# Two stages of a two-layer encoder reordered: results of a Toeplitz convolution sent from ScalarE's queue, and an output projection split into 3 + 1 + 4 heads

## The reference

```python
def conv_module(x, w_pw1, b_pw1, w_dw, b_dw, ln_g, ln_b, w_pw2, b_pw2):
    h = x @ w_pw1 + b_pw1
    h = h[..., :D_MODEL] * jax.nn.sigmoid(h[..., D_MODEL:])
    h = lax.conv_general_dilated(
        h, w_dw[:, None, :], window_strides=(1,), padding=[(CONV_HALF, CONV_HALF)],
        dimension_numbers=('NWC', 'WIO', 'NWC'), feature_group_count=D_MODEL) + b_dw
    h = jax.nn.silu(layer_norm(h, ln_g, ln_b))
    return h @ w_pw2 + b_pw2
...
    def attend(blk):
        qn, qr = blk
        s = (jnp.einsum('bqhd,bkhd->bhqk', qn, k_nope, preferred_element_type=jnp.float32)
             + jnp.einsum('bqhr,bkr->bhqk', qr, k_rope, preferred_element_type=jnp.float32))
        p = jax.nn.softmax(s * scale, axis=-1).astype(v.dtype)
        return jnp.einsum('bhqk,bkhd->bqhd', p, v)

    o = lax.map(attend, (qn_blocks, qr_blocks))
    o = o.transpose(1, 0, 2, 3, 4).reshape(B, S, N_HEADS * V_HEAD_DIM)
    return o @ w_o
```

## Time and profile before

| what | value |
|---|---|
| median of three runs | 2750.94 us |
| the profiled execution | 2742.61 us |
| its span on the core | 2740.8 us |
| TensorE matmul busy | 2650.6 us, 97% |
| VectorE busy | 1399.2 us, 51% |
| ScalarE busy | 950.8 us, 35% |
| GpSimd busy | 1576.7 us, 58% |
| mean granted clock of TensorE | 0.992 |
| convolution stage | from 550 to 820 us, about |
| last head of attention | from 2121 to 2145 us, about |

### The profile page before, as it was taken

How to read it: one execution, slowest core, us unless ns; L and a number is a source line. 1 busy time by engine, 2 the same in 40 slices (tenths; PEclk the granted TensorE clock), 3 DMA queues, 4 the chain that set the end, 5 groups by cost and what they waited for, 6 DMA issues and landing times.

```text
span 2740.8 us, 36417 instructions
## 1 busy us (share of the span) xinstructions
PE 2650.6 (97%) x14320; PEld 2470.2 (90%) x14320; DVE 1399.2 (51%) x2533; ACT 950.8 (35%) x1580; POOL 1576.7 (58%) x852
## 2 busy tenths in 40 slices
PE   7999999899899999999999999999899999999998
PEld 7899999789778899999898999998899788999998
DVE  5643333669767643333664333337766476433335
ACT  4232332444243232332432322334444242323323
POOL 2576776657443576776636866674211234768665
PEclk9999999999899999999999999999999999999999
DMA  3222221322302222221421212241000121222213
GB/s 135 75 69 70 85 77 47 125 77 91 124 39 85 80 67 72 82 77 47 162 85 62 77 58 67 77 134 72 9 24 32 70 77 70 77 62 77 82 57 123
DMA packets 61944, 210.98 MB, mean 77 GB/s; under 512 B 8016, under 2 KB 11600, under 8 KB 61776
## 3 DMA queue, kind: packets, MB, share of 16 engines
q1 hardware_dynamic: 55536, 186.54, 20.3%
q10 hardware_dynamic: 6240, 22.12, 2.1%
HBM read 193.62 MB, written 12.58 MB: 75 GB/s over the span
## 4 chain that ended last, share of the span: by engine, by line
PE 82%; DVE 11%; issue 2%; ACT 2%; POOL 2%; SPq 1%; DMA 1%; DVEq 0%; ACTq 0%; POOLq 0%
PE ps L1073 27%; PE ps L1074 26%; PE ps L1075 26%; DVE raw_sum L1749 2%; DVE sum L1749 1%; POOL pacc L1060 1%; DVE x L1767 1%; PE ps L1173 1%; DVE y L1756 1%; POOL w_lo L1020 1%; SPq L909 1%; DVE y L1773 1%; PE ps L1320 1%; PE ps L1185 0%; DVE pair L1647 0%
## 5 line engine op out<-in xcount | busy, mean ns | idle before, releaser
L1020 POOL TENSOR_TENSOR w_lo<-w_stage,w_hi 128x1024 fp32r<-128x1024 f32 (+1 forms) x455 | 1020.3, 2271 | 595.7 <-ACT w_hi L1378 589.7
L1073 PE MATMUL ps<-xn,w_hi 128*128 128x384 f32 x1920 | 646.1, 336 | 11.1 <-DVE cin L1845 5.4
L1074 PE MATMUL ps<-xn,w_hi 128*128 128x384 f32 x1920 | 644.0, 335 | 0.0
L1075 PE MATMUL ps<-xn,w_lo 128*128 128x384 f32 x1920 | 643.5, 335 | 0.0
L1378 ACT ACTIVATE w_hi<-w_stage 128x1024 fp32r<-128x1024 f32 (+1 forms) x455 | 436.0, 983 | 84.6 <-POOL w_stage L1031 54.7
L1073 PE MATMUL ps<-w_hi,hid 128*128 128x512 f32 x1056 | 413.2, 391 | 4.9 <-DVE y L1761 3.4
L1074 PE MATMUL ps<-w_lo,hid 128*128 128x512 f32 x1056 | 411.8, 390 | 0.0
L1075 PE MATMUL ps<-w_hi,hid 128*128 128x512 f32 x1056 | 411.8, 390 | 0.0
L1073 PEld LDWEIGHTS ps<-xn,w_hi 128*128 128x128 f32 x1920 | 361.9, 188 | 14.6 <-issue 13.8
L1074 PEld LDWEIGHTS ps<-xn,w_hi 128*128 128x128 f32 x1920 | 362.0, 189 | 0.8
L1075 PEld LDWEIGHTS ps<-xn,w_lo 128*128 128x128 f32 x1920 | 361.8, 188 | 0.0
(11 more groups left out here) (198 smaller groups left out, 3928.8 us busy)
## 6 DMA issues: line engine op xcount, KB each, us to landing
w_stage<-weights SPq DMA_DIRECT2D x311, 512.0 KB, 3.6
x_kept<-x ACTq DMA_DIRECT2D x18, 512.0 KB, 2.6
x<-x_kept ACTq DMA_DIRECT2D x18, 512.0 KB, 7.3
g_pre<-rows SPq DMA_DIRECT2D x7, 512.0 KB, 4.7
spread_w<-spread_in SPq DMA_DIRECT2D x6, 576.0 KB, 4.4
late_spread_w<-spread_in SPq DMA_DIRECT2D x6, 576.0 KB, 4.7
x<-x_in SPq DMA_DIRECT2D x6, 512.0 KB, 8.3
g_post<-rows SPq DMA_DIRECT2D x6, 512.0 KB, 5.4
```

The lines of the kernel that those rows point to most:

```text
L1020: pool.tensor_tensor(w_lo[:, s, 0:n], w_stage[:, s, 0:n], w_hi[:, s, 0:n].bitcast(F32), ALU.subtract).then_inc(w_split, 1)
L1073: pe.matmul(out, a[0], m[0], start=start, stop=False)
L1074: pe.matmul(out, a[0], m[1], start=False, stop=False)
L1075: return pe.matmul(out, a[1], m[0], start=False, stop=stop)
```

## The change

Convolution. The clock `pool` now also advances by 2.6 for each split that falls inside an `up`, so products are placed later. The transfers of `bring` for chunks 5 and 7 become steps of the list (`bring c a`, right after `gather c a`) and are issued by ScalarE; SyncE keeps chunk 3 and, of chunk 7, group 2. SyncE requests the first four late matrices together and the other two after the first and second `send` of chunk 7.

Attention. The output projection has three blocks: heads 0 to 2, head 3, heads 4 to 7. Nine of its groups become steps of the last head and of what follows it; the rest comes after. The last head's keys and values lie on `last_kn` and `last_val`, over parts of `lat` that are no longer read and over `act_out`, so the weight places 4 to 6 come free after head 6. Groups before the last block use PSUM banks 2 and 3. The pre-norm row that shares its place with the last head's rotated queries is loaded ahead of row unit 7 instead of 4.

```diff
+HEAD_BLOCKS = ((0, 3), (3, 1), (4, 4))
...
+    return {"ffn": FFN_BLOCKS, "conv": ROW_BLOCKS, "mla": HEAD_BLOCKS}[SUBS[b]]
...
+    return LAST_BANKS[j] if last else (2 if SUBS[b] == "mla" else 4) + j % 2
...
         def item(c, half):
+            nonlocal pool
+            at_split = s.split
             up(b, c, half)
+            pool += 2.6 * (s.split - at_split)
             pool_until(s.clock)
...
                 if r % 2 == 1:
                     on_dve(0.8, "gather", c, r // 2)
+                    if c > SPREAD_CHUNKS[0]:
+                        s.add(0, "bring", c, r // 2)
...
-        s.add(0, "bring_last")
...
+            items = [(t, h) for t in range(TILES) for h in range(2)]
+            early = iter([(0, *at) for at in items[:8]] + [(1, *items[0])] + [
+                (n, *at) for two in zip(items[8:], items[1:5]) for n, at in enumerate(two)] + [
+                (1, *at) for at in items[5:]])
...
+                if n >= QK - 6:
+                    early_down()
                 if n >= 2:
                     s.add(0.4, "probs_turn", n - 2)
                 if n >= 5 and n % 2 == 1:
                     s.add(0.6, "value", (n - 5) // 2)
+                    if n == 5 + 2 * (3 * (HEADS - 1) - 1):
+                        for i in range(4, 7):
+                            s.free(UNIT0[b] + i, "attention", 3 * (HEADS - 1))
                 s.weights()
+            early_down()
             s.add(0.6, "value", QK // 2 - 1)
-            for i in range(4, 8):
-                s.free(UNIT0[b] + i, "attention", QK // 2)
-            s.weights(until=row_unit(b, 3))
-            for t in range(TILES):
-                for h in range(2):
-                    down(b, 0, t, h, 2 * t + h)
+            s.free(UNIT0[b] + 7, "attention", QK // 2)
+            for n, t, h in early:
+                down(b, n, t, h, next(placed))
...
+        last_kn = over("last_kn", [P, 2, TOK], spot["y"] + LAT * TOK * 4, F32R)
+        last_val = [over("last_val_hi", [P, TILES, VDIM], spot["y"] + (LAT + 2) * TOK * 4, F32R),
+                    over("last_val_lo", [P, TILES, VDIM], spot["act_out"], F32R)]
...
-                    load_spread(6)
-                    load_spread(7)
+                    for g in range(LATE, GROUPS - 2):
+                        load_spread(g)
                     for r in range(PHASES):
                         send(7, r)
-                        load_spread(8 + r)
-                    bring(5)
+                        if r < 2:
+                            load_spread(GROUPS - 2 + r)
                     bring(7)
...
                 e = SPREAD_CHUNKS.index(c)
-                for a in range(2):
+                for a in range(2) if c == SPREAD_CHUNKS[0] else (1,):
                     sp.wait_ge(gathered, 2 * e + a + 1)
-                    for r in (2 * a, 2 * a + 1):
-                        if (c, r) == (KT - 1, PHASES - 1):
-                            return
+                    for r in (2 * a, 2 * a + 1) if c == SPREAD_CHUNKS[0] else (PHASES - 2,):
...
-            def bring_last():
-                act.wait_ge(gathered, 2 * len(SPREAD_CHUNKS))
-                for q in range(PHASES):
-                    act.dma_start(out_place(KT - 1, PHASES - 1, q), sums_out(KT - 1)[quarter(q), PHASES - 1, :]
-                                  ).then_inc(brought[-1], 16)
+            def bring(c, a):
+
+                e = SPREAD_CHUNKS.index(c)
+                act.wait_ge(gathered, 2 * e + a + 1)
+                for r in (2 * a, 2 * a + 1):
+                    if (c, r) == (KT - 1, PHASES - 2):
+                        continue
+                    for q in range(PHASES):
+                        act.dma_start(out_place(c, r, q), sums_out(c)[quarter(q), r, :]).then_inc(brought[e], 16)
```

More of the change, by code:

```diff
@@ L1 @@
 from contextlib import ExitStack
+from itertools import count
 import concourse.bass as bass
@@ L196, with out_bank @@
 LAST_BANKS = (4, 5, 0, 1, 4, 5, 0, 1, 2, 3, 4, 5)
-def out_bank(last, j):
-    return LAST_BANKS[j] if last else 4 + j % 2
+def out_bank(b, last, j):
+    return LAST_BANKS[j] if last else (2 if SUBS[b] == "mla" else 4) + j % 2
 def turn_bank(t):
@@ L816, in qr, with keys_of, values_of @@
             return xn[rows_, i, h + 1, cols_] if h + 1 < HEADS else qr7[i][rows_, cols_]
+        def keys_of(h, i):
+            return last_kn[:, i, :] if h == HEADS - 1 else kn[:, h % 2, i, :]
+        def values_of(h, i):
+            return last_val[i][:, :, :] if h == HEADS - 1 else val[:, h % 2, i, :, :]
         def own_rows(h):
@@ L1130, in down @@
                         pe.wait_ge(w_split, row_unit(b, c0 + nc_ - 1, h) + 1)
-                elif j == 0:
+                elif j == 0 and SUBS[b] == "conv":
                     pe.wait_ge(w_split, row_unit(b, c0 + nc_ - 1) + 1)
+                if SUBS[b] == "mla" and (n, t, h) == (0, 0, 0):
+                    pe.wait_ge(proj_done, 6 * HEADS)
                 if SUBS[b] == "ffn":
@@ L1148, in down @@
                 for k in range(nc_):
+                    if SUBS[b] == "mla" and (t, h) == (0, 0):
+                        pe.wait_ge(w_split, row_unit(b, c0 + k) + 1)
                     if SUBS[b] == "ffn" and t in (0, 3) and h == 0:
@@ L1158, in down @@
                         src, w = both(xn, c0 + k, toks(t)), unit(row_unit(b, c0 + k), h * WIDE, WIDE)
[L1159 removed]
+                    mm = mm3(ps[:, out_bank(b, last, j), :], src, w, k == 0, k == nc_ - 1)
                 mm.then_inc(out_full, 1)
@@ L1309, in score @@
                 mm3(out, [qn[:, h % 2, i, toks(t)] for i in range(2)],
-                    [kn[:, h % 2, i, ks] for i in range(2)], True, False)
+                    [keys_of(h, i)[:, ks] for i in range(2)], True, False)
                 mm3(out, [qr(h, i, slice(0, P), toks(t)) for i in range(2)], [lat[:, i, LAT - 1, ks] for i in range(2)],
@@ L1332, in value @@
                 for k in range(nk // P):
-                    mm = mm3(ps[:, 6 + j % 2, 0:2 * P], [val[:, h % 2, i, k0 // P + k, :] for i in range(2)],
+                    mm = mm3(ps[:, 6 + j % 2, 0:2 * P], [values_of(h, i)[:, k0 // P + k, :] for i in range(2)],
                              [pt[j % 2][i][:, k, :] for i in range(2)], k == 0, k == nk // P - 1)
@@ L1584, in _ @@
                     turn(*at)
-                elif kind == "bring_last":
-                    bring_last()
+                elif kind == "bring":
+                    bring(*at)
                 elif kind == "product":
@@ L1752, in down @@
                 last = n == len(blocks(b)) - 1
-                src, dst = ps[:, out_bank(last, j), :], y[:, t, half_row(h)]
+                src, dst = ps[:, out_bank(b, last, j), :], y[:, t, half_row(h)]
                 dve.wait_ge(out_full, d + 1)
@@ L1994, in proj @@
                 elif i < 4:
-                    to, src = [kn[:, h % 2, j, cols(i - 2)] for j in range(2)], ps[:, bank, 0:HALF]
+                    to, src = [keys_of(h, j)[:, cols(i - 2)] for j in range(2)], ps[:, bank, 0:HALF]
                 else:
                     t0, nt = (0, 4) if i == 4 else (4, 2)
-                    to = [val[:, h % 2, j, t0:t0 + nt, :] for j in range(2)]
+                    to = [values_of(h, j)[:, t0:t0 + nt, :] for j in range(2)]
                     src = ps[:, bank, 0:nt * P].rearrange("p (a n) -> p a n", a=nt)
```

11 lines of the change are left out of this document (7 added, 4 removed).

## The result

The changed kernel took 2723.94 us (median of four runs, 2722.29 to 2724.24); before, in the same comparison, 2750.85. The ratio is 0.9902, 95% interval 0.9885 to 0.992. The forecast was 2732.6, its range 2727 to 2743: the direction was right, the gain larger than in any case of it.

A forecast was written before the change was run, and what follows sets the result against it. TensorE, busy 97% of the span, was taken as the bound, so only its waits could be won. Convolution terms 9.0 and 6.0 plus last head 3.3 made 18.3 us, off 2750.94: 2732.6 us, range 2727 to 2743.

The forecast's parts named there:

- VectorE's list: Convolution: products placed later let sigmoids come sooner, VectorE idles less, and the last gather ends 9.0 us sooner.
- The returns: Convolution's end: ScalarE issues 24 of SyncE's 28 transfers of results, right behind their gathers; 6.0 us.
- I count no gain of clock: Convolution's end: TensorE still waits some microseconds there, so nothing was credited for a fuller granted clock.
- the late matrices' wait: Convolution: TensorE's 2.9 us for late Toeplitz matrices; the longer wait goes because they are requested ahead of the sends.
- The last head: Attention's last head: projection groups in its slots end 5.4 us of waits and add 2.1; net 3.3 us.
- Four splits now fall into this head or its end: Last head: GpSimd splits could delay VectorE's divides by 1.83 us each; nothing charged, 7.3 us if all four are exposed.
- rival C: Last head: splits hold the divides and short groups lose 2.1, costing 4.0 us more; 2739.9 us, chance 0.07.
- I keep that difference: Whole kernel: the median's 8.3 us above the profiled execution was carried over unchanged into the forecast time.
- A: Convolution: VectorE's idle only moves, through late chunk sums or a load no sooner; 2741.6 us, chance 0.13.
- B: Convolution's end: results return no faster because the transfers themselves are the limit; 2738.6 us, chance 0.10.
- D: Convolution: GpSimd becomes the bound, VectorE waits in every chunk and the kernel is slower; 2761.4 us, chance 0.04.
- E: After the changed places: a later stage absorbs the gain through a wait with its own pace; 2750.9 us, chance 0.06.

The follow-up runs named there:

- planner's clock alone: Only the `pool` advance of 2.6 per split inside an `up`, put into the kernel before: 2739.20 us, ratio 0.9970.
- second queue's run: Only the results of chunks 5 and 7 issued by ScalarE behind their gathers, put into the kernel before: 2742.01 us, ratio 0.9981.

## Why the prediction was right or wrong

**VectorE's list, 9.0 us: right.** The planner's clock alone gave 8.2, and in the first profile after, every idle came out within 0.6 us of its forecast. **The returns, 6.0: right**, 5.2 alone, and 4.0 us behind the gather where 4.1 were forecast. The whole stage gained 14.9 for 15.0 against the profile that the working started from, and 16.4 against the average of three. Two readings beside the sum were wrong: "I count no gain of clock" (5.6 of the 14.9 us are clock, within the time that VectorE's list already set), and that the late matrices' wait goes by their order (with the planner's clock alone, in the old order, 0.8 of 2.9 us is left).

**The last head, "Net 3.3 us": the step that failed.** It measured 7.7. The waits taken away (5.4) were right, the new ones 1.3 for 2.1 (0.2 us each for 0.3). What failed is the scope: the term ended with the head, though the change also moves the splits of the next network's weights, and I followed these only as far as what they could add ("Four splits now fall into this head or its end"). That two of them already held VectorE at the next entry was in the trace of before, in waits of 3.0 and 1.7 us that the text left out; rows and mechanism were those of its own warning. What was missing was 4.1 us at that entry, and the two splits put back brought 4.05 us back. The warned-of exposed divides (rival C) did not come: no divide of the last head took over 0.49 us.

**"I keep that difference": failed as well.** The 8.3 us between profile and median were read as a fixed offset, and three runs as the level. The level is 2747.2 by 77 runs, 3.7 below, and executions spread around it with the granted clock. So 4.4 (head), 3.7 (level) and 1.4 (stage C on average for stage C of the one profile used) are 9.5, of which the measured time shows 8.7. The range, widened for unknown costs alone, held nothing for either; with one of the two misses alone, the measured time would have lain inside it.

**Rivals.** A: no, VectorE waits for no later chunk sum as it does for chunk 0's, and the gather came sooner. B: no, by the second queue's run. D: no, for the same reason as A. E: no, the two stages' 24.1 us in the traces are 23.3 in the times, so later stages took nothing back that shows.

## What to carry to other kernels

When a step moves, follow what it pushes on every engine to the end of the next stage, and price what disappears there as carefully as what is added. A small VectorE operation on a chain that TensorE waits for can cost a whole GpSimd instruction if the two meet (here 2.3 us for 0.16, beside splits of 2.4); find such meetings by one operation's longest against its median. Before a few microseconds are argued from a median, run the kernel before often enough to know its own spread.

## What the runs showed of the hardware that was not expected

One program's executions on one chip spread from 2742 to 2754 us, through stretches at half clock behind waits of 2 to 7 us that hardly differ between executions: behind the same 2.96 us wait 5.2 us of clock were lost in one profile and 1.7 in another. A VectorE operation two columns wide took 2.3 us instead of 0.16 beside a GpSimd split. And the profile named a wait for several semaphores by the wrong one of them: `w_lo` for a late `xn`.
